# Sums of squares of the second norm on GpSimd instead of VectorE, in a hybrid decoder step

## What is computed

```python
def rmsnorm(x, g):
    y = xf * lax.rsqrt(jnp.mean(xf * xf, axis=-1, keepdims=True) + EPS)
    return (y * g.astype(jnp.float32)).astype(x.dtype)

xn = rmsnorm(h, g_mix)                                  # first norm
h = h + mix @ w_out                                     # mix: state-space heads and window attention
h = h + cross_attention(rmsnorm(h, g_cross), mem_k, mem_v, w_cq, w_co)   # second norm
hn = rmsnorm(h, g_ffn)                                  # third norm
h = h + (jax.nn.silu(hn @ w_gate) * (hn @ w_up)) @ w_down
y_prompt = rmsnorm(hp, g_final)                         # final norm
```

## Time and profile before

| | us |
|---|---|
| median of 3 runs | 3255.36 (3254.73 to 3258.53) |
| the profiled execution, its own time | 3259.13 |
| its span, first to last instruction | 3257.4 |
| PE busy | 3017.2 (93% of the span) |
| DVE busy | 1466.7 (45%) |
| ACT busy | 1122.9 (34%) |
| POOL busy | 1023.9 (31%) |
| mean granted TensorE clock | 0.929 of 2.4 GHz |

### The profile page before, as it was taken

The page is one execution under the profiler, slowest core; times in us unless marked ns, Lnnn a source line. Parts: engine busy times, 40 slices in busy tenths (PEclk is TensorE's granted clock), DMA queues, the critical chain, the costliest instruction groups (busy, mean ns, idle before and its releaser), DMA issues. The chain is left out here.

```text
span 3257.4 us, 35782 instructions
## 1 busy us (share of the span) xinstructions
PE 3017.2 (93%) x13972; PEld 2415.7 (74%) x13972; DVE 1466.7 (45%) x2221; ACT 1122.9 (34%) x1816; POOL 1023.9 (31%) x507
## 2 busy tenths in 40 slices
PE   8886999999999999999999999999779999667898
PEld 6664887877887878778778787788658888565752
DVE  5464555656246556563465565634342232313111
ACT  3433364344234543442335434423332222111100
POOL 3200433333443333334433333343214444410000
PEclk9996999999999999999999999999889999656679
DMA  5453422222335222223352322233313333571256
GB/s 144 125 95 103 126 74 84 75 65 82 99 103 164 77 85 75 65 79 98 107 164 72 90 67 70 78 97 114 113 38 98 97 97 91 148 212 43 65 182 222
DMA packets 490989, 332.44 MB, mean 102 GB/s; under 512 B 58559, under 2 KB 458051, under 8 KB 490806
## 3 DMA queue, kind: packets, MB, share of 16 engines
q1 hardware_dynamic: 486318, 323.74, 34.0%
q10 hardware_dynamic: 1880, 6.34, 0.5%
q0 software_dynamic: 2624, 0.09, 0.1%
HBM read 309.86 MB, written 21.23 MB: 102 GB/s over the span
## 5 line engine op out<-in xcount | busy, mean ns | idle before, releaser
L786 POOL TENSOR_TENSOR w_lo<-w_raw,w_hi 128x1024 fp32r<-128x1024 f32 x400 | 970.5, 2429 | 1713.3 <-ACT w_hi L800 1713.3
L1547 PE MATMUL L<-xa_h,w_hi 128*128 128x512 f32 x1536 | 614.1, 400 | 3.9 <-DVE xa_l L1370 3.9
L1548 PE MATMUL L<-xa_h,w_lo 128*128 128x512 f32 x1536 | 602.7, 392 | 0.0
L1549 PE MATMUL L<-xa_l,w_hi 128*128 128x512 f32 x1536 | 602.4, 392 | 0.0
L800 ACT ACTIVATE w_hi<-w_raw 128x1024 fp32r<-128x1024 f32 x400 | 421.0, 1053 | 438.3 <-PE L L1549 431.8
L1547 PEld LDWEIGHTS L<-xa_h,w_hi 128*128 128x128 f32 x1536 | 291.2, 190 | 76.3 <-issue 11.4
L1549 PEld LDWEIGHTS L<-xa_l,w_hi 128*128 128x128 f32 x1536 | 290.9, 189 | 62.2
L1548 PEld LDWEIGHTS L<-xa_h,w_lo 128*128 128x128 f32 x1536 | 291.4, 190 | 59.6 <-issue 1.0
L1506 DVE TENSOR_TENSOR sg<-sg,L 128x512 f32<-128x512 f32 x88 | 60.6, 688 | 531.5 <-PE L L1549 531.5
L1547 PE MATMUL L<-hid_h,w_hi 128*128 128x512 f32 x704 | 280.4, 398 | 6.1 <-DVE hT L1514 6.1
L1549 PE MATMUL L<-hid_l,w_hi 128*128 128x512 f32 x704 | 275.3, 391 | 0.0
(11 more groups left out here) (488 smaller groups left out, 4440.1 us busy)
## 6 DMA issues: line engine op xcount, KB each, us to landing
w_raw<-in_w_gate_dram SPq DMA_DIRECT2D x88, 512.0 KB, 3.8
w_raw<-in_w_up_dram SPq DMA_DIRECT2D x88, 512.0 KB, 3.8
w_raw<-in_w_down_dram SPq DMA_DIRECT2D x88, 512.0 KB, 3.4
w_raw<-in_w_in_dram SPq DMA_DIRECT2D x56, 512.0 KB, 3.8
xt<-xT_dram SPq DMA_DIRECT2D x48, 256.0 KB, 4.1
wS<-in_w_down_dram SPq DMA_DIRECT2D x11, 1024.0 KB, 5.0
wS<-in_w_gate_dram SPq DMA_DIRECT2D x10, 1024.0 KB, 5.0
wS<-in_w_up_dram SPq DMA_DIRECT2D x10, 1024.0 KB, 5.0
```

The lines of the kernel that those rows point to most:

```text
L786: pool.tensor_tensor(w_lo[:, n % RING, 0:w], w_raw[:, n % RING, 0:w], w_hi[:, n % RING, 0:w].bitcast(F32), ALU.subtract)\
L1547: pe.matmul(acc, wh, rh, start=(k == 0), stop=False)
L1548: pe.matmul(acc, wl, rh, start=False, stop=False)
L1549: last = pe.matmul(acc, wh, rl, start=False, stop=(k == kn - 1))
```

## The change

The eight sums of squares of each block's second norm go from DVE to POOL. There the sum of tile i stands in front of the split of panel w0+4+i. The sums of the third and of the final norm stay on DVE.

```diff
             @blk.gpsimd
             def _(pool):
+                def sum_squares(b, n):
+                    i = KT * 3 * b + n
+                    pool.wait_ge(s["sq_done"], i + 1)
+                    if n == 0:
+                        ins = pool.tensor_copy(sqsum[:], sq[:, 0, :])
+                    else:
+                        pool.wait_ge(s["sqsum_done"], i)
+                        ins = pool.tensor_tensor(sqsum[:], sqsum[:], sq[:, n % 2, :], ALU.add)
+                    ins.then_inc(s["sqsum_done"], 1)
+
...
+                    for b in range(NBLK):
+                        w0 = pos[("W", b, 0)]
+                        if w0 + 4 <= n < w0 + 4 + KT:
+                            sum_squares(b, n - w0 - 4)
                     pool.wait_ge(s["hi_ready"], n + 1)
...
                             dve.tensor_tensor(hT[:, i, :], bank(bank_of[o]), src, ALU.add)\
                                .then_inc(s["ev_D"], 1)
-                            if i >= 1:
-                                sum_squares(b, 0, i - 1)
...
-                    sum_squares(b, 0, KT - 1)
                     if more:
                         window(b + 1, WIN1)
```

## The result

The changed kernel took 3271.66 us, the median of 8 runs (3267.33 to 3274.14), against 3258.27 us of the kernel before on the same chip (8 runs, 3253.70 to 3265.98). The ratio is 1.0037 with a 95% interval of 1.0028 to 1.0046: **12.0 us slower** (9.1 to 15.0), where +11.1 was forecast. The profiled execution took 3273.58 us for a span of 3271.9 us.

What follows compares the result with a forecast made beforehand. It took PE, busy 93% of the span, as the bound. Terms −6.0 + 4.6 + 8.5 + 4.0 = +11.1 us on 3255.36 gave 3266.5 us, range 3257 to 3273 (the forecast's own range 3261 to 3272).

Steps and rivals of the forecast that it cites:

- Term 1: W stage, blocks 1 and 2: without the sums the `xb_l` waits and the W6 wait go, −6.0 us.
- without it a step of DVE is 2.65 us: DVE's W-stage step, 5.31 us, loses the sum's 2.66 us, leaving some 2.8 us to spare per panel.
- DVE without idle time in the W stage: Sign in the changed kernel's profile that the prediction is wrong; it expected DVE idle between its steps.
- late tiles: `xt` tiles loaded behind W7; would cost up to 1.3 us in block 1, counted as nothing behind a late W4.
- Rival 2: DVE's two-input operations wait for splits and POOL's sums: 6.3 us a step, W6 wait returns, +4.5, 3271 us; 15%.
- Term 2: POOL's first sum delays W4's split: 3.3 us block 1, 2.3 block 2, less 1.0 for earlier stores, +4.6 us.
- place A: POOL's order before the split of W4, where the first sum waits for the first square; +4.6 us (0.7 to 5.6).
- Term 3: Token sums wait for POOL's last sum: 2.2 us in blocks 0 to 2, 3.4 in block 3, less 1.5; +8.5 us.
- place B: POOL's order before the split of w0+11, where the last sum stands behind the split of w0+10; +8.5 us (7 to 10).
- Term 4: PE's clock falls to 1.2 GHz after new waits, about two falls at 2 us: +4.0 us (0 to 7).
- three new chances: New half-clock stretches possible after W4's waits in blocks 1 and 2 and in block 0; about two expected, 2 us each.
- Rival 1: Not slower: stores land 2.5 us sooner, the first sum's wait costs 0.7 instead of 4.6 us, 3255 to 3257 us; 15%.

Runs made afterwards that it cites:

- narrow_adds: The changed kernel with its 28 adds on POOL over 8 columns instead of 512, order and waits kept: 3262.6 us.
- last_early: The changed kernel with the sum of tile 7 moved in front of the split of w0+10, beside that of tile 6: 3262.2 us.
- both_ends: The changed kernel with tile 0's sum behind the split of W4 and tile 7's in front of the split of w0+10: 3258.9 us.
- first_late: The changed kernel with the sum of tile 0 moved behind the split of W4: 3272.8 us, and 3269.3 us in a second set.
- last_on_dve: The changed kernel with each block's last sum (tile 7) back on VectorE, sums 0 to 6 staying on GpSimd: 3265.8 us.

## Why the prediction was right, point by point

- **Against the forecast.** The time lies in the range, near its upper end. Of the 5.2 us between 3271.66 and the forecast of 3266.5, 2.9 are the kernel before, whose median of 8 runs came out higher than that of the 3 runs the forecast started from.
- **Term 1, −6.0 us for the waits of `xb_l` and W6: mis-sized, −3.9.** PE still waits 0.30 and 1.88 us for `xb_l` (W6's 0.85 is gone). The step that failed is "without it a step of DVE is 2.65 us", so that 2.8 us are to spare. It took the hold-up for a property of the sum. It belongs to the first operation with two SBUF inputs that comes after a split starts: with the sum away, `xt` takes 2.29 us instead of 0.74, then `xa_l` waits for POOL's own sum, and the step is 5.13 us. The prediction named DVE without idle time in the W stage as a sign of being wrong, and this sign came: after the first `xa_l` DVE stands still in block 1 for 0.22 us and for the late `xt` tiles (2.13 and 0.39), in block 2 for such tiles alone (1.44 and 0.32). So the time was right while the mechanism of this term was not. The late tiles, which the prediction put at nothing behind a late W4, cost PE nothing at W6, but they start DVE's chain late; narrow_adds shows that a chain with short steps makes it up. Rival 2 had this mechanism; its price (6.3 us a step, and 15.6 us in all against the forecast's starting point) was too high, since of each hold-up only the part behind the start counts, and its W6 wait didn't return. The rule of the Trainium skill that was cited with it (Perfetto Trace Analysis, Optimizing Scalar/DVE Operations) held here: offloading between the two did not help.
- **Term 2, +4.6 us at place A: measured 4.8** (3.27 in block 1, forecast 3.3; 1.53 in block 2, forecast 2.3; none in block 3). Its account (`put_y` held by the store, the first square, the copy, the split) stands in the rows above. Of the 1.0 us taken off for stores that land sooner, half came: `put_y` starts 24.2 us after W0 in block 1, as before the change, and 22.2 instead of 22.6 in block 2. The experiments add what the text didn't say: a third to a half of this wait is one that the k panel would otherwise have (two thirds, 3.1 of 4.6 us, from last_early to both_ends).
- **Term 3, +8.5 us at place B: measured 8.9.** 2.23, 2.48, 2.48 and 6.71 us of waits, less the 3.52 of before in block 3 and the 1.49 for `diag` in block 0, which is gone as forecast. last_early shows that this term, with the clock behind it, is most of the change's cost.
- **Term 4, +4.0 us of clock: measured about 2.6.** 21.8 us at half clock against 16.7 (10.5 and 6.2), half of the difference being lost. Of the three new chances one fell, after W4's wait of 3.27 us in block 1; after 2.23 us in block 0 and 1.53 us in block 2 PEclk stayed at 1.00. Block 3's stretch grew instead, from 6.2 to 7.5 us.
- **The sum:** −3.9 + 4.8 + 8.9 + 2.6 = +12.4 us, beside +13.1 in the stages and +12.0 in the medians. The forecast's +11.1 was near partly by luck: term 1 was 2.1 us too good, and the clock 1.4 us too dear. The price of an add, 1.25 us, was measured as 1.25 to 1.30 where DVE is quiet. By the figure in the Trainium skill's GPSIMD Engine Reference (section 3.1) it would be an estimated 1.1 us, less than any add of 512 columns took here.
- **Rival 1** (not slower) needed the stores to land 2.5 us sooner. They landed at the same time after W0 in block 1 and 0.5 us sooner in block 2.

Three questions stay open. What the 3 to 5 us are that first_late shows in the stages and not in the medians wasn't settled. No kernel loads the `xt` tiles ahead of W7, which would part the late tiles from the lock. And no kernel was tried in which the splits themselves are cut in two, which would bound every hold-up.

## What to carry to other kernels

When an instruction looks long because it waits for another engine's port, taking it away hands the wait to the next one that needs the port: price the hold-up by what follows in the queue, and test it by making the instruction tiny, not by removing it. A piece of work that is put into an engine's fixed order costs what stands ahead of it there, and of a series it is the last piece, whose result another engine waits for, that needs the best place: no engine waited for the results of the sums before it here, and the last cost 9 us of waits. A late piece also delays the loads that wait for the same queue, as the `xt` tiles show. Before moving work from a chain without idle time, look at what makes the chain start late: a reorder of a few lines on a third engine gave 6 us where the move could not.

## What the runs showed of the hardware

- VectorE's operations with two SBUF inputs and GpSimd's splits and adds exclude each other for their whole length, in both directions: 8 columns on VectorE take 2.21 us instead of 0.15 beside a split, and on GpSimd 0.65 instead of 0.20; GpSimd's 512-column add takes 1.75 us instead of 1.26, its split up to 2.89 instead of 2.40. An operation with one input in PSUM is not held: `hT` takes its 0.68 us at 1007.14, inside the split of 1006.60 to 1009.48. The Trainium skill's page SBUF — State Buffer (Who interferes with whom) calls the port pair that the two engines share "an exclusive lock", and says that a VectorE instruction with two SBUF inputs contends with a GpSimd one that reads SBUF; these rows agree.
- Two inputs are not needed. The cast of `k_l`, 128 columns with one SBUF input, takes 0.22 us where GpSimd is idle, and 2.39 beside the split of 1021.98 to 1024.81 (both in the kernel after):

```profile
367.09 0.22 DVE L1178 CAST k_l<-k_l 128x128 fp32r<-128x128 f32 x1
...
1022.51 2.39 DVE L1178 CAST k_l<-k_l 128x128 fp32r<-128x128 f32 x1
```

- TensorE's clock did not fall after every wait: 1.53 us (block 2) and 2.23 us (block 0) of idle time left it at 2.4 GHz, waits of 2.48 and 3.27 us were followed by 1.2 GHz for 3.1 to 6.3 us. The length of the last wait alone does not decide it: in block 1 of last_on_dve a wait of 1.80 us, which ended 2.8 us after one of 0.28 had, was followed by this stretch:

```profile
1022.90:1028.00 5.10, 5.06 (x16) 0.50 0.86 189
```
